# Layer 0's input projection begun on the left half of the columns, with six modulation blocks beside it and none beside the output projection

## What is computed

```
mod = silu(c) @ w_ada[l] + b_ada[l]
sh1, sc1, g1, sh2, sc2, g2 = split(mod, 6)
h = rmsnorm(x, norm1_g[l]) * (1 + sc1) + sh1
z = h @ w_in[l]                      # columns: u, v (gMLP), q, k, v (attention)
out_a = gmlp_mixer(u, v, ...)        # a 128x128 lower-triangular matrix for each of 8 groups
out_b = diff_attention(q, k, v, ...) # 4 heads, two softmax maps each
x = x + g1 * (concat(out_a, out_b) @ w_out[l])
h = rmsnorm(x, norm2_g[l]) * (1 + sc2) + sh2
x = x + g2 * mixer(h)                # layer 0: dense SwiGLU; layer 1: top-2 of 8 experts
```

## Time and profile before

| | |
|---|---|
| median of 3 executions | 1326.3 us (1324.92 to 1326.74) |
| profiled execution | 1324.67 us, its span 1322.9 us |
| PE busy | 1252.5 us, 95% of the span |
| DVE, ACT, POOL busy | 82%, 62%, 4% |
| 16 transfer engines | 409.61 MB, mean 310 GB/s |
| granted TensorE clock | mean 0.985 of full speed |

### The profile page before, as it was taken

How to read it: one execution, slowest core, us unless ns; L and a number is a source line. 1 busy time by engine, 2 the same in 40 slices (tenths; PEclk the granted TensorE clock), 3 DMA queues, 4 the chain that set the end, 5 groups by cost and what they waited for, 6 DMA issues and landing times.

```text
span 1322.9 us, 17505 instructions
## 1 busy us (share of the span) xinstructions
PE 1252.5 (95%) x5463; PEld 879.7 (66%) x5463; DVE 1078.4 (82%) x1383; ACT 817.6 (62%) x1167; POOL 56.4 (4%) x75
## 2 busy tenths in 40 slices
PE   5999969999989898999999999999999999999996
PEld 1445757777767676777676676676676676776664
DVE  2857777888779756788988998988988988988896
ACT  3125434444444544677877777777777777777774
POOL 2102000000000021000000000000000000000000
PEclk8999989999999989999999999999999999999999
DMA  9997639888857535699999999999999999999991
GB/s 294 387 387 244 216 131 317 282 281 298 316 207 262 159 96 179 230 358 365 371 361 365 364 367 367 357 367 367 362 366 369 357 366 368 363 370 368 373 368 60
DMA packets 277871, 409.61 MB, mean 310 GB/s; under 512 B 6676, under 2 KB 209436, under 8 KB 277572
## 3 DMA queue, kind: packets, MB, share of 16 engines
q1 hardware_dynamic: 273732, 393.82, 86.8%
q0 software_dynamic: 4096, 15.25, 3.5%
HBM read 401.70 MB, written 7.34 MB: 309 GB/s over the span
## 4 chain that ended last, share of the span: by engine, by line
PE 68%; SPq 15%; DVE 9%; issue 4%; ACT 2%; DMA 2%; DVEq 0%; POOL 0%; ACTq 0%; POOLq 0%
PE bank L1776 19%; PE bank L1777 19%; PE bank L1778 18%; SPq L598 13%; PE bank L1916 5%; DVE w_lo L1185 3%; DVE ada_acc L1237 1%; DMA raw<-in_w_ada 1%; DVE more_lo L1185 1%; SPq L582 1%; DMA raw<-in_moe_w_up 1%; ACT w_hi L773 1%; PE bank L1804 1%; PE bank L1811 1%; PE bank L2215 1%
## 5 line engine op out<-in xcount | busy, mean ns | idle before, releaser
L1185 DVE TENSOR_TENSOR w_lo<-raw,w_hi 128x1024 fp32r<-128x1024 f32 x366 | 444.9, 1221 | 87.5 <-ACT w_hi L773 84.6
L773 ACT ACTIVATE w_hi<-raw 128x1024 fp32r<-128x1024 f32 x366 | 381.7, 1051 | 101.0 <-PE bank L1778 93.1
L1185 DVE TENSOR_TENSOR more_lo<-raw,more_hi 128x1024 fp32r<-128x1024 f32 x264 | 308.2, 1218 | 2.8 <-ACT more_hi L773 2.8
L773 ACT ACTIVATE more_hi<-raw 128x1024 fp32r<-128x1024 f32 x264 | 260.2, 1047 | 0.1
L1776 PE MATMUL bank<-more_hi,hgT_hi 128*96 128x512 f32 x368 | 149.7, 407 | 2.1 <-DVE more_lo L1185 2.1
L1776 PE MATMUL bank<-w_hi,hT_hi 128*128 128x512 f32 x320 | 136.3, 426 | 15.4 <-DVE hT_lo L1272 9.9
L1777 PE MATMUL bank<-more_hi,hgT_lo 128*96 128x512 f32 x368 | 144.9, 394 | 0.0
L1778 PE MATMUL bank<-more_lo,hgT_hi 128*96 128x512 f32 x368 | 144.7, 393 | 0.0
L1776 PE MATMUL bank<-w_hi,hgT_hi 128*96 128x512 f32 x336 | 132.6, 395 | 0.0
L1777 PE MATMUL bank<-w_hi,hgT_lo 128*96 128x512 f32 x336 | 132.6, 395 | 0.0
L1237 DVE SCALAR_TENSOR_TENSOR ada_acc<-raw,silu_c,ada_acc 128x512 f32<-128x512 f32 x152 | 113.9, 749 | 22.3 <-DMA raw<-in_w_ada 15.5
(11 more groups left out here) (276 smaller groups left out, 1718.1 us busy)
## 6 DMA issues: line engine op xcount, KB each, us to landing
raw<-in_moe_w_gate SPq DMA_DIRECT2D x88, 1024.0 KB, 11.3
raw<-in_moe_w_up SPq DMA_DIRECT2D x88, 1024.0 KB, 13.6
raw<-in_moe_w_down SPq DMA_DIRECT2D x88, 1024.0 KB, 11.9
raw<-in_w_ada SPq DMA_DIRECT2D x48, 1024.0 KB, 11.0
raw<-in_w_in SPq DMA_DIRECT2D x20, 1024.0 KB, 11.5
raw<-in_ffn_w_gate SPq DMA_DIRECT2D x11, 1024.0 KB, 5.5
raw<-in_ffn_w_up SPq DMA_DIRECT2D x11, 1024.0 KB, 8.1
raw<-in_ffn_w_down SPq DMA_DIRECT2D x11, 1024.0 KB, 11.2
```

Source lines behind the costliest of these rows:

```text
L773: act.activation(like(hi_of(s)), src, ACT.Copy).then_inc(hi_done, 1)
L1185: dve.tensor_tensor(like(lo_of(s)), src, like(hi_of(s).bitcast(F32)), ALU.subtract).then_inc(split_done, 1)
```

## The change

`chunk_stream` now sends the weights of the left half first: blocks 0 and 1 (scale and shift, left), the first chunk of q, block 2, the first chunk of k, block 3, then the second chunks of q and k, each followed by a whole modulation block; blocks 4 to 9 all come before the last piece. The pieces of layer 0 run in the order of `IN_PIECES`: both left pieces of q and k first. Block 2 is taken by DVE alone (`FIRST_TILE`), DVE does all four scalings and shifts of h, and POOL's early loads wait for `ada_out` 4, that is for the first four blocks. `in_bank` and `qk_bank` get other banks in layer 0 so that q and k can be open together.

```
+FIRST_TILE = [2, 2, 0, 2]
+IN_PIECES = [[(0, 0), (0, 1), (1, 0), (1, 1), (0, 2), (0, 3), (1, 2), (1, 3)] + [(t, s) for t in range(2, 5) for s in range(4)],
...
+IN0_DONE = [3, 4, 6, 8, 10]
...
-BESIDE_OUT = [(0, 9), None]
...
# GpSimd
             pool.wait_ge(consts, 6)
+            pool.wait_ge(ada_out, 4)
...
-            shift_h(0, h_tok, SH1)
...
# ScalarE
-                    if piece >= 4 and piece % 4 == 0:
+                    if layer == 0 and piece in (4, 7, 11, 13, 16, 18):
+                        modulation_next()
...
# VectorE, start
+            ada_half(0, (2, 3))
+            ada_half(1, (2, 3))
+            modulation_out(1)
+            ada_half(0, (2, 3))
+            ada_half(1, (2, 3))
+            first_scaled(0)
+            modulation_out(2)
+            first_shifted(0)
             transposed(0, 0)
-            modulation_out()
+            ada_half(0, range(4))
+            ada_half(1, range(4))
+            modulation_out(3)
+            first_scaled(1)
+            ada_half(0, (2, 3))
+            ada_half(1, (2, 3))
+            modulation_out(4)
+            first_shifted(1)
+            transposed(0, 1)
...
# VectorE, pieces
+                    if piece == (8, 7)[layer]:
+                        mixer_rows()
+                    if layer == 0 and piece < 12:
+                        if piece >= 4:
+                            ada_half(piece % 2, range(4))
+                    elif layer == 0 or BESIDE_IN[layer][t]:
                         ada_half(half, (2 * q, 2 * q + 1))
-                    if piece == 3 and layer == 0:
+                    if piece == 6 and layer == 0:
                         lambda_dots()
-                    if piece == 7:
-                        mixer_rows()
                     if piece == 11:
                         dve.wait_ge(qk_mm, 4 * layer + NT + 1)
...
# VectorE, output projection
-                if BESIDE_OUT[layer]:
-                    ada_half(0, (0, 1))
...
-                    modulation_out()
                     out_update(BY_TILE, 1)
...
# TensorE
-            for n in range(4):
+            for n in range(2):
                 for half in range(2):
-                    if (n, half) == (3, 1):
-                        h_transposes(0, 0, 0)
                     ada_first(n, half)
+            h_transposes(0, 0, 0)
...
+                    t, sub = IN_PIECES[layer][piece]
+                    if layer == 0 and piece == 2:
+                        ada_first(2, 0)
+                        ada_first(2, 1)
+                    if layer == 0 and piece == 3:
+                        ada_first(3, 0)
+                        ada_first(3, 1)
+                    if piece == (7, 5)[layer]:
+                        pe.wait_ge(q_out, NT * (layer + 1))
+                        ada_sum()
+                    if piece in (9, 13) or (layer, piece) == (0, 11):
                         pe.wait_ge((q_out, k_out, v_out)[t - 1], NT * (layer + 1))
                         ada_sum()
...
+                        if piece == 4:
                             h_transposes(0, 0, 1)
...
-                    if piece == 3:
+                    if piece == (8, 3)[layer]:
                         mixer_turned()
-                    if piece == 5:
+                    if piece == (7, 5)[layer]:
                         pe.wait_ge(q_out, NT * (layer + 1))
                         turned(layer, 0)
...
-                if BESIDE_OUT[layer]:
-                    ada_sum()
```

More of the change, by code:

```diff
@@ L87, in chunk_stream @@
             for half in range(2):
+                if (layer, half) == (0, 0) and t < 2:
+                    continue
                 s.append(("in", layer, j, half))
-                if BESIDE_IN[layer][t]:
+                if layer == 0 and t < 3:
+                    s += [("ada", *BESIDE_IN[0][t if t < 2 else 2 + half], both) for both in range(2)]
+                elif layer == 0:
+                    s.append(("ada", *BESIDE_IN[0][t + 1], half))
+                elif BESIDE_IN[layer][t]:
                     s.append(("ada", *BESIDE_IN[layer][t], half))
         s += [("out", layer, 0, 1), ("out", layer, 1, 1)]
-        for j in range(2):
-            if BESIDE_OUT[layer]:
-                s.append(("ada", *BESIDE_OUT[layer], j))
-            s.append(("out", layer, j, 0))
+        s += [("out", layer, 0, 0), ("out", layer, 1, 0)]
         if layer == 0:
@@ L326, in mod_block, with in_bank @@
             return mod[:, piece, CB * half:CB * half + CB]
-        def in_bank(t, a):
+        def in_bank(layer, t, a):
+            if layer == 0 and t == K_AT:
+                return bank[2 + a]
             return bank[(2 * t + a) % 3]
@@ L334, in score_bank, with qk_bank @@
             return bank[3 + 2 * (h % 2) + m]
-        def qk_bank(part, a):
+        def qk_bank(layer, part, a):
+            if layer == 0 and part == 0:
+                return bank[6 + a]
             return bank[(3, 6, 4, 5)[2 * part + a]]
@@ L362, in sum_bank @@
                 return bank[7 - i % 2]
+            if (layer, j) in BESIDE_IN[0]:
+                return bank[(0, 0, 0, 2, 7, 7)[BESIDE_IN[0].index((layer, j))]]
             if (layer, j) in BESIDE_IN[layer][:3]:
@@ L905, in _ @@
                     std_of_rows(0, h_tok)
-                    for i in range(2, 5):
-                        bias(i)
+                    bias(2)
+                    bias(3)
                     transposed(0, 0)
+                    bias(4)
                     bias(5)
@@ L913, in block_done @@
                     if layer == 0:
[L914 removed]
+                        act.wait_ge(in0_used, IN0_DONE[t])
                     else:
@@ L983, in _ @@
                 for piece in range(20):
-                    if piece >= 4 and piece % 4 == 0:
+                    if layer == 0 and piece in (4, 7, 11, 13, 16, 18):
+                        modulation_next()
+                    if layer and piece >= 4 and piece % 4 == 0:
                         if BESIDE_IN[layer][piece // 4 - 1]:
@@ L1311, in beside @@
             def beside(i, piece):
[L1313 to L1316, removed]
+                if i and piece == 2:
                     tile_lo(i, 1, 1)
@@ L1347, in _ @@
                 dve.wait_ge(ada_out, ada_no[0])
-                if layer == 0:
-                    norm(0, SC1, SH1, h_tok, range(2, 4))
                 def block_done(t):
                     if layer == 0:
-                        dve.wait_ge(in0_used, 2 * (t + 1))
+                        dve.wait_ge(in0_used, IN0_DONE[t])
                     else:
@@ L1526, in _ @@
                     out_lo(piece)
-                    if piece < 6 and BESIDE_OUT[layer]:
-                        ada_half(1, (0, 1) if piece == 4 else (2, 3))
                     if piece == 5:
-                        modulation_out(ada_no[0] - (1 if BESIDE_OUT[layer] else 0))
-                dve.wait_ge(ada_out, ada_no[0] - (1 if BESIDE_OUT[layer] else 0))
+                        modulation_out()
+                dve.wait_ge(ada_out, ada_no[0])
                 if layer == 0:
@@ L1903, in bank_free @@
                 def bank_free(t, a):
+                    if layer == 0 and t == K_AT:
+                        return
                     done = (q_out, k_out, v_out, g_out)
@@ L1925, in split_piece @@
                         cols = slice(CB * kk, CB * kk + CB)
-                        last = three(in_bank(t, a)[:, :], hT_hi[:, k, P * a:P * a + P],
+                        last = three(in_bank(layer, t, a)[:, :], hT_hi[:, k, P * a:P * a + P],
                                      hT_lo[:, k, P * a:P * a + P], hi_of(s)[:, cols], lo_of(s)[:, cols],
@@ L1986, in _ @@
                     if sub == 0:
-                        if t >= 2 and BESIDE_IN[layer][t - 2]:
+                        if t >= (3, 2)[layer] and BESIDE_IN[layer][t - 2]:
                             pe.wait_ge(ada_out, ada_no[0])
```

90 lines of the change are left out of this document (46 added, 44 removed).

## The result

| | before | changed |
|---|---|---|
| median of 12 runs, us | 1326.25 (1324.12 to 1328.08) | 1328.16 (1327.29 to 1330.49) |
| ratio to before | 1 | 1.0023 [1.0015, 1.0032] |
| profiled execution, us | 1324.67 | 1327.85 |

The changed kernel is 1.9 us slower by the medians, 3.1 us by the ratio (0.0023 x 1326.25). The profiled executions differ by 3.2 us, as do the spans. 1327.7 was predicted.

The account below looks back on a forecast made before the run. PE was taken as the bound from 42.95 us on, waiting for weights before that. Terms -1.7 + 1.6 + 0.9 + 1.4 - 0.8 = +1.4 us took the median from 1326.3 to 1327.7 us; range 1321.5 to 1332.0.

Parts of the forecast that it names:

- The loads that POOL issues: At the kernel's start: moving these loads away brings the fourth weight chunk 5.3 us sooner (2.2 to 7.0).
- rival D: Slower: the move of the loads is worth only their bytes at the start; +3.4 us, 1329.7; chance 0.13.
- The left half and piece 4: Layer 0's start: first product at 28.3 us instead of 42.95, piece 4 at 48.9, 9.8 us earlier.
- The second gap's clock: PE idle from 24.3 to 26.3 us, before the left half's transposes: no cost, +1.6 us at its high end.
- To the scores: Layer 0, piece 4 to scores: DVE holds scores until 81.0 us (79.9 to 82.5), 1.7 us earlier than before.
- F: Reordering takes nothing off the path, landing times alone set the scores (82.5 us): +2.9 us, 1329.2; chance 0.08.
- The clock: Behind PE's idle gap of some 7 us before scores, matmuls run at lower level: +1.6 us (0 to 2.9).
- B: Clock stays up behind the gap or the stall on v doesn't come: -0.1 us, 1326.2, no change; chance 0.13.
- Scores to piece 13: Layer 0: block 6's sum before piece 11, +0.9 us; PE's stall on v in piece 12, +1.4 us (0 to 2).
- Edits with one answer: Different banks, `IN0_DONE`, ACT's order: nothing; POOL's loads start at about 44.7 us, `subln` lands near 61, against 64.4.
- E: Loads collide with chunks, mixer weights or lambdas 2 to 4 us late before piece 8: +4.4 us, 1330.7; chance 0.06.
- C: Faster: start gains 7.0 us, moved loads cost only bytes, clock holds, v in time: -4.4 us, 1321.9; chance 0.22.

## Why the prediction was right, and where its terms were off

The time came within 0.5 us of the forecast (1328.16 against 1327.7) and inside the likeliest case's own range, by the chain that was forecast. That it came so near is partly luck: the terms as the profile has them add up to -1.0 + 2.9 + 0.9 + 1.4 - 0.85 = +3.4 us, as the profiled pair differs (3.2), and not to +1.4; the medians happen to lie only 1.9 apart. The difference from before was forecast as +1.4 us and measured as +1.9 (medians) to +3.1 (ratio). 0.23%, with 0.15 to 0.32 as its interval, lies across the 0.2% that was taken as the border, so "no change" is not what the best estimate says; the forecast stood on the low side. Term by term:

| step | predicted | measured in the profile |
|---|---|---|
| fourth chunk in hand | 21.4 (-5.3) | 19.5 (-7.15) |
| first product | 28.3 | 26.5 |
| piece 4 | 48.9 | 49.1 |
| mixer weights done | 66.4 | 66.8 |
| chunk for piece 10 | 73.9 | 74.4 |
| scores | 81.0 (-1.7) | 81.7 (-1.0) |
| the clock behind the gap | +1.6 | +2.9 |
| block 6's sum | +0.9 | +0.9 |
| gap on v | +1.4 | +1.4 |
| output projection | -0.8 | -0.85 |

- **The loads that POOL issues.** The start gained 7.15 us; I took 5.3 and gave 7.0 as the most. The row with four slices at 11 to 49 GB/s was the better witness: what the loads cost is the standstill beside them, and the queue's own share (5.2 us) leaves that out. So rival D, which took only their bytes (2.2 us), is out. The estimate of 2.0 us by the Trainium skill (DMA: Bandwidth & Descriptors, "Anatomy of one DMA — SWDGE (gpsimd) path") is as far off: that rule prices such a transfer, not what it does to others.
- **The left half and piece 4.** The start was 1.8 us better than forecast and piece 4 was not, for the first two pieces took 8.80 us and not 7.1. The second gap's clock, which I put at nothing with +1.6 at the high end, was at the high end. Two errors cancelled.
- **To the scores.** DVE was the bound, as written: 66.8, then 74.4, then the copy. Yet two terms behind it were off, and cancelled. The chunk in hand at 74.4 is the twenty-first of the stream; in the old timing it was due one chunk (2.7 us) after the row at 73.20, at 75.9. So of the stream's lead of 7.15 us (5.3 in the forecast) 1.5 was left (2.0 in the forecast), and the moved loads cost some 5.6 us there, more than the 2.2 to 5.2 given for them. The queues say the same: from 43.0 to 62.1 us SP's queue moved 4.62 MB instead of 6.61, which is 5.1 us at 387 GB/s. In the old order with late loads the lead shrank alike, from 6.9 at the fourth chunk to 1.7 at the twentieth (71.51 against 73.20), and PE kept its 7.0 us, for it waited for no chunk. F (landing times alone) fell: with the copy ahead of the tiles the scores started at 73.25.
- **The clock** is the step that was mis-sized: "+1.6, with 0 at the low end and 2.9 at the high end". It was 2.9 in the profiled execution, shown by the kernel that kept PE busy, and 3.7 and 4.2 in two others with such a gap, beyond the high end. I had carried over the cost behind 5.37 us, where eight products ran slow; here 16 short score products, their masks and part of piece 10 did. B, in which the clock stays up or v doesn't stall, is out: both came.
- **Scores to piece 13.** Sum and gap came as worked out, with DVE's copy of v as releaser. -1.0 + 2.9 + 0.9 + 1.4 = 4.2 of the measured 4.5 us; the last 0.3 were not traced.
- **Edits with one answer.** POOL's loads started at 45.4 (44.7 forecast), `subln` was no releaser anywhere, and E (mixer weights late) didn't come.
- **C** had its first condition, the full 7.0 us at the start, but not the clock and not v.

The working never asked what the first term was worth without the others: a part worth 5.6 to 6.8 us (the late loads alone) was a plain gain, and the copy's place, costed as it stood, took 8 to 9.

## What to carry to other kernels

On an engine that works through its queue in order, put the copy that releases another engine ahead of bulk work with slack: eight tiles in front of one 0.7 us copy cost 8 to 9 us here. When a change has several parts, read what each is worth to the stage's bound alone; here one part (small loads issued behind the start) held all of the gain that is clear of noise and could be had without the rest. A gap on PE costs itself and then the lower clock behind it: 2.9 us behind 7.4, and up to 4.2 behind 8.2.

## What the hardware did that was not expected

**Small loads hold up large ones.** 0.85 MB from POOL's queue kept the fourth 1 MB chunk back by 7 us at the start, with slices of 11 to 49 GB/s while chunks were queued. That their place is the cause is shown by moving them back alone in the new order and, with what needs them, later in the old one. Moved to 45 us, they make the same standstill at 52 us, and it costs the stream nearly as much (5.6 us); it is cheap only because nothing on PE's path waits for a chunk there, but for the 1.19 us that DVE waits at 74.40 in the changed kernel. Not every load from POOL does this: from 43.0 to 62.1 us in the kernel before, its queue moved 0.79 MB while the engines kept 388 GB/s. What in the early group of eight loads makes the standstill stays open.

**Short gaps, either clock.** The gap before the left half's transposes is 2.04 us in the changed kernel and in that with the early copy of k. Behind it the same 16 products took 8.80 us in the first and 7.11 in the second, though no edit lies ahead of it. Layer 1's scores show it between two executions of one kernel, the kernel before with late loads (PE, first run, then second):

```profile
425.78 0.93 PE L1865 MATMUL bank<-kT,qT 64*128 64x128 f32 x8 [1.51 <-DVE kT L1462]
```

```profile
424.58 1.65 PE L1865 MATMUL bank<-kT,qT 64*128 64x128 f32 x8 [2.29 <-DVE kT L1462]
```

The next 20 us, in the kernel that kept PE busy (gap 2.29) and in the kernel before (gap 1.50):

```profile
432.36:452.36 20.00, 19.88 (x87) 14.60 (x88) 11.94 (x31) 6.87 (x20) 0.00 (x0) 0.83 0.66 211
```

```profile
432.61:452.61 20.00, 19.87 (x101) 14.66 (x101) 14.24 (x35) 9.55 (x29) 0.00 (x0) 1.00 0.68 211
```

0.83 against 1.00 over 20 us is 3.4 us of PE's time, in a stage that no edit touched. The kernel that kept PE busy gained 3.2 us at `y_scaled` (160.89 against 164.12) and had 0.4 left at the router.

One gap further up decides between the two. All twelve traces have a gap of 2.83 to 2.85 us some 30 us earlier. In the same two executions (PE, first run, then second):

```profile
395.81 0.79 PE L1777 MATMUL bank<-w_hi,hT_hi 128*128 128x512 f32 x1 [2.83 <-DVE hT_lo L1273]
```

```profile
395.28 0.50 PE L1777 MATMUL bank<-w_hi,hT_hi 128*128 128x512 f32 x1 [2.83 <-DVE hT_lo L1273]
```

Where the products behind it ran slowly (first row 0.79 or 0.80 us, seven traces), the gap before layer 1's scores was 1.50 or 1.51 us, at full clock. Where they ran at full clock (0.50, five traces), PE was done sooner, the later gap was 2.28 or 2.29, and the lower clock came there. So one slow stretch takes the place of the other, and the net is about 2 us, not 3.4: from `y_scaled` to the router 355.1 to 356.6 us in the seven, 357.6 to 358.4 in the five. That is as much as the effect of this change, and it is why single profiles here can't be compared end to end. Why a gap of 2.83 us, or of 2.04, has either clock behind it stays open.

The Trainium skill (TensorE: Matmul & The Clock Gate, "What's actually happening") says of the slow products at a kernel's start that their number varies from run to run and that they cost under 1% of a typical span. The stretches here lie behind gaps in the middle of the kernel, and the traces have the same picture: 3.4 us are 0.26%.
